# Four producers of a fused transformer kernel: moved in their queue, or their consumer's wait divided

## What is computed

```python
o_cmp, o_slc = nsa_cmp_slc(q, kcmp, vcmp, ks, vs)
o_win = banded_attention(q, kw, vw, B_WINDOW, WIN_QBLOCK)
o = g[0] * o_cmp + g[1] * o_slc + g[2] * o_win
return (o * silu(z)) @ w_out
```

## Time and profile before

| what | value |
|---|---|
| median of 3 runs | 2399.9 us |
| the profiled execution | 2403.05 us |
| its span, first to last instruction | 2401.2 us |
| TensorE matmuls busy | 2318.4 us (97%) |
| VectorE busy | 1460.2 us (61%) |
| ScalarE busy | 1074.3 us (45%) |
| GpSimd busy | 66.8 us (3%) |
| DMA | 474.84 MB, mean 198 GB/s |
| mean granted TensorE clock | 0.992 |

### The profile page before, as it was taken

The page is one execution under the profiler, slowest core; times in us unless marked ns, Lnnn a source line. Parts: engine busy times, 40 slices in busy tenths (PEclk is TensorE's granted clock), DMA queues, the critical chain, the costliest instruction groups (busy, mean ns, idle before and its releaser), DMA issues.

```text
span 2401.2 us, 30849 instructions
## 1 busy us (share of the span) xinstructions
PE 2318.4 (97%) x12120; PEld 1867.5 (78%) x12120; DVE 1460.2 (61%) x2171; ACT 1074.3 (45%) x1598; POOL 66.8 (3%) x90
## 2 busy tenths in 40 slices
PE   4999999999998999999999999999999999999998
PEld 2777786766776878888888888788887887788977
DVE  2344455666687776766755555664677545468875
ACT  3443234444433364444443443454555454456654
POOL 2000000111000000000000000000000000000000
PEclk9999999999999999999999999999999999999999
DMA  9755645677778756676665555555434565433233
GB/s 322 252 188 198 208 145 195 223 258 259 259 268 304 270 193 227 228 252 221 230 220 184 185 192 189 162 176 191 158 119 130 192 224 182 152 112 97 95 127 123
DMA packets 234708, 474.84 MB, mean 198 GB/s; under 512 B 7624, under 2 KB 10032, under 8 KB 233312
## 3 DMA queue, kind: packets, MB, share of 16 engines
q1 hardware_dynamic: 230736, 456.16, 56.2%
q0 software_dynamic: 3536, 16.94, 2.1%
q10 hardware_dynamic: 320, 0.13, 0.0%
HBM read 471.10 MB, written 2.10 MB: 197 GB/s over the span
## 4 chain that ended last, share of the span: by engine, by line
PE 85%; DVE 6%; DMA 5%; ACT 2%; issue 2%; SPq 0%; POOL 0%; DVEq 0%; POOLq 0%; ACTq 0%
PE acc L1753 22%; PE acc L1755 22%; PE acc L1754 22%; DMA raw<-in_w_mod 3%; PE acc L2167 2%; PE acc L2169 2%; PE acc L2170 2%; DVE wlo L1030 2%; PE acc L2211 1%; PE turn L2225 1%; PE acc L1789 1%; PE aux L2245 1%; ACT whi L561 1%; DMA raw<-in_w_o 1%; DMA raw<-in_w_b_up 1%
## 5 line engine op out<-in xcount | busy, mean ns | idle before, releaser
L1030 DVE TENSOR_TENSOR wlo<-raw,whi 128x1024 fp32r<-128x1024 f32 x674 | 820.7, 1224 | 746.1 <-ACT whi L561 741.5
L561 ACT ACTIVATE whi<-raw 128x1024 fp32r<-128x1024 f32 x674 | 708.6, 1058 | 995.7 <-PE acc L1755 834.9
L1753 PE MATMUL acc<-whi,xhi 128*128 128x512 f32 x1536 | 614.0, 400 | 17.3 <-DVE wlo L1030 9.9
L1755 PE MATMUL acc<-whi,xlo 128*128 128x512 f32 x1536 | 602.0, 392 | 0.0
L1754 PE MATMUL acc<-wlo,xhi 128*128 128x512 f32 x1536 | 601.4, 392 | 0.0
L1753 PEld LDWEIGHTS acc<-whi,xhi 128*128 128x128 f32 x1536 | 290.6, 189 | 101.4 <-issue 27.8
L1755 PEld LDWEIGHTS acc<-whi,xlo 128*128 128x128 f32 x1536 | 290.1, 189 | 62.1
L1754 PEld LDWEIGHTS acc<-wlo,xhi 128*128 128x128 f32 x1536 | 290.9, 189 | 58.3 <-issue 0.5
L1753 PE MATMUL acc<-whi,hhi 128*128 128x512 f32 x512 | 201.5, 394 | 2.0 <-DVE hlo L1051 2.0
L1755 PE MATMUL acc<-whi,hlo 128*128 128x512 f32 x512 | 199.4, 389 | 0.0
L1754 PE MATMUL acc<-wlo,hhi 128*128 128x512 f32 x512 | 199.3, 389 | 0.0
(11 more groups left out here) (323 smaller groups left out, 2409.8 us busy)
## 6 DMA issues: line engine op xcount, KB each, us to landing
raw<-in_w_ff SPq DMA_DIRECT2D x128, 1024.0 KB, 5.2
raw<-in_w_mod SPq DMA_DIRECT2D x96, 1024.0 KB, 7.6
raw<-in_w_in SPq DMA_DIRECT2D x64, 1024.0 KB, 5.7
raw<-in_b_w_in SPq DMA_DIRECT2D x45, 1024.0 KB, 5.0
raw<-in_a_w_in SPq DMA_DIRECT2D x36, 1024.0 KB, 5.1
raw<-in_w_o SPq DMA_DIRECT2D x16, 1024.0 KB, 5.3
raw<-in_a_w_out SPq DMA_DIRECT2D x16, 1024.0 KB, 5.1
raw<-in_b_w_out SPq DMA_DIRECT2D x16, 1024.0 KB, 5.0
```

What stands on the lines that cost most here:

```text
L561: act.activation(whi[:, k % 2, on], raw[:, n % 4, on], ACT.Copy).then_inc(hi_ready, 1)
L1030: dve.tensor_tensor(wlo[:, k % 2, on], raw[:, LOAD_OF_UNIT[k] % 4, on], whi[:, k % 2, on].bitcast(F32), ALU.subtract)\
L1753: pe.matmul(bank, hi[:, tile(kt), tok], w_hi, start=kt == k_first, stop=False, skip_group_check=True)
L1755: mm = pe.matmul(bank, lo[:, tile(kt), tok], w_hi, start=False, stop=kt == k_first + UK * k_units - 1, skip_group_check=True)
```

## The change

The memset and the reduction stand ahead of the splits of layer b's units 3 to 14 in VectorE's program. The spread of the norm comes after step 11, ahead of the rotation there. At the first head TensorE waits for one product less, and for the last one only ahead of the conditioning. In every quarter of the MLP the call for each of the units of blocks 1 to 3 is divided into its two halves, and in the last one the rows are turned between the halves of the second unit, not after the first unit.

```diff
@@ -1657,6 +1657,9 @@
         norms(2, RMS["b"])
+        dve.memset(cols1[:, 0:KVG * 2 * NC], 0.0).then_inc(zeroed, 1)
+        dve.tensor_reduce(same_head, ident[0:HG * NC, 0:HG * NC].rearrange("p (h n) -> p h n", h=HG), AX.X, ALU.add)\
+           .then_inc(zeroed, 1)
         split(UNIT["b_att"] + 3, 3)
         split(UNIT["b_att"] + 6, 9)
@@ -1676,8 +1679,6 @@
-            elif kind == "norm":
-                spread_norm(ATTN["b"])
@@ -1689,9 +1690,6 @@
         keys_of = lambda n: kv6[:, :, n * 256:(n + 1) * 256]
-        dve.memset(cols1[:, 0:KVG * 2 * NC], 0.0).then_inc(zeroed, 1)
-        dve.tensor_reduce(same_head, ident[0:HG * NC, 0:HG * NC].rearrange("p (h n) -> p h n", h=HG), AX.X, ALU.add)\
-           .then_inc(zeroed, 1)
@@ -1701,6 +1699,8 @@
             if u in STEPS:
                 step(*STEPS[u])
+            if u == 11:
+                spread_norm(ATTN["b"])
             if u % 4 == 3:
@@ -1939,8 +1939,10 @@
                 if k == 0:
-                    pe.wait_ge(acc_freed, plus(g0, 1, h))
+                    pe.wait_ge(acc_freed, g0 + h - (h == 0))
                 multiply(u0 + k, k, 4, 0, i=h, per=4)
+                if (h, k) == (0, 0):
+                    pe.wait_ge(acc_freed, g0)
                 condition(COND["att"] + k, k, acc[:, 2, :], h, 4, 8)
@@ -2105,9 +2107,10 @@
                 for k in range(2):
-                    multiply(u0 + 8 + 2 * n + k, k, 2, 2 * (n % 2), 0, hhi, hlo, e, 16)
-                    if last and k == 0:
-                        turn_rows("a", res3, (2 * n - 2, 2 * n - 1), ready=lambda g: pe.wait_ge(res_done, g // 2 + 1))
+                    for tiles in ((0, 1), (2, 3)):
+                        multiply(u0 + 8 + 2 * n + k, k, 2, 2 * (n % 2), 0, hhi, hlo, e, 16, tiles=tiles)
+                        if last and k == 1 and tiles[0] == 0:
+                            turn_rows("a", res3, (2 * n - 2, 2 * n - 1), ready=lambda g: pe.wait_ge(res_done, g // 2 + 1))
```

## The result

The changed kernel takes 2386.0 us (median of 5 runs, 2385.3 to 2389.1) against 2399.9 us before (5 runs beside it, 2399.1 to 2400.6): ratio 0.9943, 95% interval 0.9932 to 0.9954. It is 13.9 us faster, where 16.1 were forecast. The profiled execution took 2389.14 us, 2387.3 us of it the span.

What follows compares the result with a forecast made beforehand. TensorE, busy 97% of the span, bounds the kernel; gains lie in its waits and low clock. 4.75 + 4.42 + 4.37 + 2.58 = 16.1 us off 2403.05, less 3.15, gives 2383.8 us; range 2381 to 2389.

Steps and rivals of the forecast that it cites:

- the attention: First head's wait for banks (L1942): dividing it gains 4.75 us, 3.09 of wait and 1.66 of low clock.
- the zeroed pairs: TensorE's wait for the memset and reduction (L1692, L1693): moving them gains 4.42 us, about 2.9 wait and 1.54 low clock.
- the norm: TensorE's wait for the spread norm's copy (L1500) at L2139: spreading it earlier gains 4.37 us.
- the turning: Last quarter of the MLP: turns half a unit later remove three of four waits, 0.86 us each, 2.58 us.
- the second rival: Weights' DMA paces the stage from 650 to 770 us and swallows the attention's 4.75 us: 2388.5 us; chance 0.07.
- the fourth: Rival: dividing L2108's call stops the stream in all eight quarters, 48 units, costing 41.3 us: 2425 us, slower; chance 0.02.
- The third rival: Last quarter: the later turn finds its next wait at once and the 2.58 us come back: 2386.4 us; chance 0.04.
- The low clock: TensorE's clock falls behind the waits of 2.9, 2.7 and 2.6 us, lengthening following units by 1.5 to 1.7 us.
- The first rival: Low clock isn't tied to the three waits and comes anyway; 4.8 us stay, time 2388.6 us; chance 0.07.
- less 3.15: Last step of the sum: 2386.9 us less the profiled execution's 3.15 us above the median gives 2383.8 us.
- so a gain is passed on: Behind each place, semaphores order work and DMA issues that move along, so the gains of 16.1 us reach the end.

Runs made afterwards that it cites:

- the fourth turn: The changed kernel with the turn of pairs 6 and 7 also put half a unit later, into layer a's product; 2385.6 us, ratio 0.9937.
- the turning alone: The kernel before with only the last quarter's turns moved half a unit later and the MLP calls divided; 2398.9 us, ratio 0.9995.
- the attention alone: The kernel before with only the first head's wait for banks divided; 2394.8 us, ratio 0.9983.
- the zeroed pairs alone: The kernel before with only the memset and the reduction moved ahead of the splits; 2396.4 us, ratio 0.9983.
- the filled norm: The kernel before with 10 unread matmuls ahead of TensorE's wait for the spread norm; 2400.5 us, ratio 0.9994.
- the delay of 5 us: The changed kernel with 21 unread matmuls (4.8 us) ahead of the first slab's transposes in the attention; 2390.1 us, ratio 0.9953.
- the filling: The changed kernel with 45 unread matmuls (8, 12, 19 and 6) in the four remaining waits between 670 and 845 us; 2383.9 us, ratio 0.993.

## Why the prediction was right

**The waits, term by term.** Right. The idle parts, as the runs separate them, are 3.19 us at the attention (3.09 forecast), 2.97 at the zeroed pairs (2.9) and 2.92 at the norm (2.77); the turning gave 2.74 (2.58). That is 11.8 us of sure gain. "Behind each place everything is ordered by semaphores of work that moves along with it" held: the stage of 650 to 770 us kept its distance from the attention, which disposes of the second rival, and the division of L2108's call cost nothing over 42 units, which disposes of the fourth. The third rival is out as well: the later turn finds no wait, and even the fourth turn fits.

**The low clock.** The mechanism was right and its size wrong. Where it comes at one of the three places it costs 1.6 us, as taken from the rows (once, in the turning alone, the norm's was shorter, and the place took 10.40 us instead of 10.64). But the prediction booked it in full at all three places, because the one profiled execution had it at all three. Over the profiled executions that keep these waits it shows in 5 of 6 at the attention, in 4 of 5 at the zeroed pairs, and in 2 of 4 at the norm: 11 of 15. On average the three places were worth 4.8 x 11 / 15 = 3.5 us of low clock. The first rival (the low clock comes anyway) is out as it stands, since the clock is 1.00 wherever the wait went, but right in part: the low clock isn't tied to these waits alone. In the profiled execution after, the places at 672 and 843 us took over.

**The steps that failed are in the sum.** It took 16.1 us off the profiled execution and then "less 3.15" to come to the median. But that execution stood 3.15 us above the median partly because all three places were low in it. One cannot take off the low stretches of an unlucky execution and its bad luck too. The 31 runs of the kernel before bear this out: those with a mean granted clock of 0.992 took 2400.7 to 2403.6 us, those with 0.994 or 0.995 took 2397.4 to 2400.2. Without the last subtraction the sum reads 2386.9, against a measured 2386.0 and 2386.6. That closeness is in part luck: against the profiled execution after, 2389.14 us, the same sum is 2.2 us too low. The second step that failed is "so a gain is passed on", which took the return for nothing: about 1 us came back.

**What was given back.** The four profiled executions with the attention's edit, nothing ahead of it and no filling (the changed kernel twice, the attention alone, the fourth turn) need 491.0 to 492.3 us from the condition to the wait at 861 to 866 us; the six without it need 490.2 to 491.0. The means are 491.4 and 490.5, so about 1 us comes back in that stretch. It sits behind the wait of L2009 at 769 us: from its end to that of the wait at 843 us it is 73.4 to 73.6 us in those four, and 72.4 to 72.6 in five of the six. What goes with it: where TensorE has lost 1.6 us at 672 us, it comes late to the wait near 757 us (3.0 us idle instead of 3.9), runs 8 or 9 matmuls low behind it instead of 13, then waits 5 us at 769 us instead of 4 and runs 6 to 8 low there instead of 2 to 4. So much of what the low stretch at 672 us cost was taken up by the next wait: in the profiled execution after, condition to 757 us is only 0.35 us longer than before. The sixth kernel, the zeroed pairs alone, has just this pattern without the attention's edit, and reads 73.3; but the filled norm was low at 673 us too and reads 72.6. Why the place at 672 us is low in all four and in only two of the six others isn't settled; behind the delay of 5 us it was full, which hints at when TensorE arrives, but one kernel doesn't show it.

**The account.** 11.8 of waits + 3.5 of low clock - 1.0 given back = 14.3 us; measured 13.9, twice. The 3.5 and the 1.0 are estimates from one or two profiled executions of each kernel.

**The yardstick of "what would show it".** Slab to condition 6.2 us, clock 1.00 behind the three places, one wait for L1450, the eight quarters unchanged: all as written.

## What the runs showed that was not expected

**A low stretch looks much the same each time, and doesn't come each time.** Behind a wait of 1.8 to 2.9 us at the three places of the change and near 672 and 843 us either nothing happens, or the clock is low over 3.2 to 3.7 us, beginning 0 to 1.6 us after TensorE starts again: 7 or 8 matmuls run 0.43 us apart instead of 0.23, or at the norm the four transposes and 6 matmuls. Behind one such wait it was shorter (2.9 us, the norm's in the turning alone, where it had begun before TensorE started again). The odds differ by place: the 1.82 us at 843 us had it once in 12 profiled executions, the waits of 2.5 to 5.2 us near 757 and 769 us each time they weren't filled. The 2.2 us of idle time that the filling left near 769 us were followed by 1.00 both times. The Trainium skill (TensorE: Matmul & The Clock Gate, section "What's actually happening") says that the unit which judges TensorE's activity looks at windows that run on their own and don't start with the kernel, so that the place of a change of clock varies from run to run. That fits one program being low at 843 us once and not the other time. Its advice on idle gaps (section "Why this matters for your kernels"), which the prediction set against the rows, names gaps longer than the waits of 1.8 to 2.9 us: the runs show that these cost too, only not each time.

**A copy on VectorE takes longer beside GpSimd.** The moved copy of L1500, forecast at 0.29 us, takes 1.14 in the changed kernel; timeline of GpSimd and VectorE there:

```profile
2074.52 1.12 POOL L534 TENSOR_TENSOR qkv<-qkv,lam 120x512 f32<-120x512 f32 x1 [60.85 <-ACT qkv L991]
2074.65 1.14 DVE L1500 COPY arena<-silu_c 128x256 f32<-128x256 f32 x1
```

It starts 0.13 us after the multiplication on GpSimd and ends 0.15 us after it. It is 1.13 or 1.14 us in all nine profiled executions with the edit, and 0.28 or 0.29 in the five with it in its old place, where GpSimd does nothing. The kernel before has the like elsewhere: a TENSOR_SCALAR of 60x256 (L1685) takes 0.67 us at 2021.75, beside a DMA issue of GpSimd that lasts to 2022.33, and 0.29 us at 2064.65 without one. The Trainium skill (SBUF — State Buffer, section "SBUF: two separate sides") says that VectorE and GpSimd share a pair of ports, held for the whole instruction by whichever starts first, the other being blocked; for VectorE it names operations in a 2-port mode, or with two inputs in SBUF against a GpSimd operation that reads SBUF. The two ends agree with that; in which mode the copy ran no run shows. Nothing on TensorE's path waited for the rotation behind it, so the 0.85 us were free here.

## What to carry to other kernels

Price a wait in two parts: its idle time, which is sure, and the low clock behind it, which is worth its 1.6 us only as often as it shows, and only where no later wait takes it up; one profiled execution doesn't tell how often, several do. If the terms of a sum are taken from one execution, don't also subtract that execution's distance to the median. Where a wait can't be removed, unread matmuls that end before the releaser kept the clock up here: four such fillings gave 2.7 us.
